# The stick-breaking mask: added in PSUM by VectorE instead of multiplied in by TensorE

## The chip, the cores and the metric

One NeuronCore of a Trainium2 chip runs one launch of the kernel. The metric is the device time in microseconds (us). Engines are named as the profile names them: TensorE (PE, its weight loads PEld), VectorE (DVE), ScalarE (ACT), GpSimd (POOL) and SyncE (SP, which here only issues DMAs).

## What is computed

A hybrid decoder layer over 512 tokens of 1024 channels, in float32. The part that the change touches is the stick-breaking branch of the attention: 8 heads of 64 channels, causal and strict (a token doesn't see itself).

```
z = q @ k.T * HEAD_DIM ** -0.5
strict = k_pos[None, :] < q_pos[:, None]
log_one_minus = where(strict, log_sigmoid(-z), 0.0)
suffix = reverse_cumsum(log_one_minus) - log_one_minus
weights = where(strict, exp(log_sigmoid(z) + suffix), 0.0)
out = weights @ v
```

Beside it stand a forgetting attention (Fox, also 8 heads, softmax with a bias of cumulative log forget gates, s <= t), the projection `x @ W_in` that makes q, k, v and the gates, the merge of both branches by gates, `W_out` and a LayerNorm, and then a feed-forward part (up projection, depthwise convolution, gelu, down projection, LayerNorm).

## The kernel before

**Products.** Every float32 operand is split in a high and a low part (`*_hi`, `*_lo`, type fp32r), and a product is three matmuls (hi hi, hi lo, lo hi; `split_product`). ScalarE writes the high parts of the weights (`high_in_order`), GpSimd the low parts (`w_lo`, L414). Weights stream in blocks of 128x1024 through four slots; SyncE loads the next block when TensorE has finished the one in its slot (`block_done`).

**Halves.** The attention runs as 8 halves, h = 0 to 7. A half is one head of each branch; two halves (e = 0, 1) make a pair of heads, and a pair's q and k rows are made while the halves before it run. Each engine has its program of a half written out by hand, and semaphores join them. In its half TensorE does, in this order: stick-breaking scores into PSUM columns 0 to 1279 (`SB_PS`), a piece of the projection (`fill(1)`), Fox scores (columns from `FX_PS`), `fill(2)`, transposes of the Fox weights (L1076), `fill(3)`, transposes of the stick-breaking weights, `fill(4)`, then the products of both branches' weights with v. The fills are the blocks of `x @ W_in` for the gates and for the next pair's q and k: 12 matmul triples in `fill(2)`. A fill's bank must have been read before it is written again (`block_read`, ScalarE: `g_all` L524 or `qk_t` L509).

**Scores.** The four query blocks r = 3, 2, 1, 0 have 512, 384, 256 and 128 keys, so a pass is four matmuls of 1280 columns in all. There are two passes: in the stick-breaking branch one with 128 rows (`sb_q`, `sb_k`: high parts stacked with low parts) and one with 64 rows (`qk_lo` with `sb_k`), in the Fox branch two with 128 rows. After each pass the mask -1e30 is added on the diagonal blocks by matmuls of `ident_bf` with `mask_bf` (`masked`, L1046): one of 256 columns after the first pass, two of 128 after the second.

**After the stick-breaking scores** (`sb_scored`) ScalarE runs Abs, Relu, Exp and Ln over 128x1280 (L544 to L549), and VectorE makes the sums (`sb_sums`, L800). VectorE's program of a half from h = 1 on is: Fox maxima (`fx_max`, L792; ScalarE needs them for the Exp into `fx_p`, L555), `sb_sums`, normalising `fx_p`, the difference L823, the split of the next pair's q and k in odd halves (`split_next`, L757 and L693), low parts of both branches' weights (L693), and at the end for b = 1 (Fox) and then b = 0 (stick-breaking) the sum of the head's output and its split (L844, L847, L693). In half 0 `sb_sums` stands ahead of `fx_max`, and ahead of both stands the split of pair 0, which ends with `fx_k` (L693).

**The stack.** When a pair's split is done (`qk_split`), SyncE copies rows from one half of the partitions to the other with four DMAs per branch (`stack`, L341 and L342: `fx_q`, `fx_k`, twice). TensorE waits for the Fox stack of a pair before the Fox scores of the pair's first half (`stack_in[1]`).

Of the kernel before, what the change touches and what calls it, by code (L numbers as in the profile page):

```python
# [21 lines left out]
P = 128  # L22
# [15 lines left out]
HALVES = 2 * PAIRS  # L38
# [76 lines left out]
def layer(nc, xT, x_tok, w_stream, w_out, cols, rows, square, out):  # L115
# [11 lines left out]
    def at(name, shape, dt, offset):  # L127
        return nc.alloc_sbuf_tensor_at(name, shape, dt, offset=offset)
# [72 lines left out]
    ident = at("ident", [P, P], f32, area_c + 2048 + 576)  # L201
    ident_bf = at("ident_bf", [P, P], bf16, area_c + 2624 + 1536)
    mask_bf = at("mask_bf", [P, 2, 2, P], bf16, area_c + 2624 + 1792)
    small = area_c + 2624 + 2816
    q_bias = at("q_bias", [P, 4 * PAIRS], f32, small)
    fx_nmax = at("fx_nmax", [P, SB], f32, small + 64)
# [16 lines left out]
    with ExitStack() as ctx:  # L223
# [5 lines left out]
        SB_PS, FX_PS = 0, 3 * 512  # L229

        def sem(name):
            return ctx.enter_context(nc.semaphore(name))
# [24 lines left out]
        v_hi_done, v_split = sem("v_hi_done"), sem("v_split")  # L257
        sel_ready = sem("sel_ready")
        sb_scored, sb_turned, sb_mixed = sem("sb_scored"), sem("sb_turned"), sem("sb_mixed")
        sb_absed, sb_relued, sb_exped, sb_lned = sem("sb_absed"), sem("sb_relued"), sem("sb_exped"), sem("sb_lned")  # L260
        sb_summed, sb_logged, sb_weighed = sem("sb_summed"), sem("sb_logged"), sem("sb_weighed")
        sb_w_hi, sb_w_split = sem("sb_w_hi"), sem("sb_w_split")
# [197 lines left out]
        def _(act):  # L460
# [75 lines left out]
            def half(h):  # L536

                pair, e = h // 2, h % 2
                scores = ps[:, SB_PS:SB_PS + FLAT]

                if h > 0:
                    act.wait_ge(sb_mixed, h)
                act.wait_ge(sb_scored, h + 1)
                nc.scalar.activation(sb_t[:], scores, ACT.Abs).then_inc(sb_absed, 1)  # L544
                nc.scalar.activation(sb_r[:], scores, ACT.Relu).then_inc(sb_relued, 1)
                act.wait_ge(sb_absed, h + 1)
                nc.scalar.activation(sb_t[:], sb_t[:], ACT.Exp, scale=-1.0).then_inc(sb_exped, 1)
                act.wait_ge(sb_exped, h + 1)
                nc.scalar.activation(sb_t[:], sb_t[:], ACT.Ln, bias=1.0).then_inc(sb_lned, 1)  # L549
                if h > 0:  # L550
                    act.wait_ge(o_split[1], h)
                act.wait_ge(fx_maxed, h * SB + SB)
                for r in range(SB):
                    off, width = QUERY_OFF[r], P * (r + 1)
                    nc.scalar.activation(fx_p[:, off:off + width], ps[:, FX_PS + off:FX_PS + off + width], ACT.Exp,  # L555
                                         bias=fx_nmax[:, r:r + 1],
                                         accum_out=fx_sum[:, r:r + 1]).then_inc(fx_exped, 1)
                fill(h, 0)
                if e == 0:

                    if h > 0:
                        act.wait_ge(fx_mixed, h)
                    for b in range(2):
                        nc.scalar.activation(v_parts[:, b, :, :, 0, :], v_of_pair(pair, b),
                                             ACT.Copy).then_inc(v_hi_done, 1)

                act.wait_ge(sb_logged, h + 1)
                nc.scalar.activation(sb_t[:], sb_t[:], ACT.Exp).then_inc(sb_weighed, 1)

                act.wait_ge(fx_turned, h + 1)  # L570
                nc.scalar.activation(fx_hi[:], ps[:, FX_PS:FX_PS + FLAT], ACT.Copy).then_inc(fx_w_hi, 1)
                fill(h, 1)
                if len(FILLS[h]) == 4 and h != TAIL:
                    fill(h, 2)
                act.wait_ge(sb_turned, h + 1)
                nc.scalar.activation(sb_hi[:], scores, ACT.Copy).then_inc(sb_w_hi, 1)
                last = 3 if len(FILLS[h]) == 4 and h != TAIL else 2
                read_fill(h, last)

                for b, mixed in ((1, fx_mixed), (0, sb_mixed)):  # L580
                    place = 512 * MIXED_BANKS[h][b]
                    act.wait_ge(mixed, h + 1)
                    if b == 0 and h > 0:
                        act.wait_ge(o_split[0], h)
                    nc.scalar.activation(o_low[b][HEAD_DIM * e:HEAD_DIM * (e + 1), :],
                                         ps[HEAD_DIM:P, place:place + 512], ACT.Copy).then_inc(o_low_done[b], 1)
                high_in_order(FIRST[h] + last + 3)
                if h == TAIL:
                    fill(h, 3)
# [101 lines left out]
        def _(dve):  # L691
# [13 lines left out]
            nc.vector.tensor_copy(ident_bf[:], sq_raw[:, 0, :])  # L705
            for side in range(2):
                nc.vector.tensor_copy(mask_bf[:, :, side, :], sq_raw[:, 1:3, :])
            nc.vector.memset(ln_eps[:], LN_EPS)
            nc.vector.memset(f_zero[:], 0.0).then_inc(const_ready, 1)
            dve.wait_ge(vb_in, 16)  # L710
# [84 lines left out]
            def sb_sums(h):  # L795
                dve.wait_ge(sb_relued, h + 1)
                dve.wait_ge(sb_lned, h + 1)
                for r in range(SB):
                    keys = slice(QUERY_OFF[r], QUERY_OFF[r] + P * (r + 1))
                    nc.vector.tensor_tensor_scan(sb_t[:, keys][:, ::-1], sb_t[:, keys][:, ::-1], sb_r[:, keys][:, ::-1],  # L800
                                                 0.0, ALU.add, ALU.add).then_inc(sb_summed, 1)

            def half(h):
                pair, e = h // 2, h % 2

                if h == 0:
                    sb_sums(h)
                    fx_max(h)
                else:
                    fx_max(h)  # L810
                    sb_sums(h)

                dve.wait_ge(fx_exped, h * SB + SB)
                if h > 0:
                    dve.wait_ge(fx_normed, h * SB)
                nc.vector.reciprocal(fx_rec[:], fx_sum[:]).then_inc(fx_inverted, 1)
                dve.wait_ge(fx_inverted, h + 1)
                for r in range(SB):
                    off, width = QUERY_OFF[r], P * (r + 1)
                    nc.vector.tensor_scalar(fx_p[:, off:off + width], fx_p[:, off:off + width],  # L820
                                            fx_rec[:, r:r + 1], None, ALU.mult).then_inc(fx_normed, 1)
                dve.wait_ge(sb_summed, (h + 1) * SB)
                nc.vector.tensor_tensor(sb_t[:], ps[:, SB_PS:SB_PS + FLAT], sb_t[:],  # L823
                                        ALU.subtract).then_inc(sb_logged, 1)

                if h < HALVES - 1:
                    select_bias(h + 1, 1 - e)
                split_next(h, 0)

                dve.wait_ge(fx_w_hi, h + 1)  # L830
                split_lo(fx_lo[:], ps[:, FX_PS:FX_PS + FLAT], fx_hi[:]).then_inc(fx_w_split, 1)
                split_next(h, 1)
                split_next(h, 2)

                dve.wait_ge(sb_w_hi, h + 1)
                split_lo(sb_lo[:], ps[:, SB_PS:SB_PS + FLAT], sb_hi[:]).then_inc(sb_w_split, 1)
                split_next(h, 3)

                rows_ = slice(HEAD_DIM * e, HEAD_DIM * (e + 1))
                for b in (1, 0):  # L840
                    place = 512 * MIXED_BANKS[h][b]
                    o_hi, o_lo = oT_hi[rows_, pair + PAIRS * b, :], oT_lo[rows_, pair + PAIRS * b, :]
                    dve.wait_ge(o_low_done[b], h + 1)
                    nc.vector.tensor_tensor(o_sum[b][rows_, :], ps[0:HEAD_DIM, place:place + 512],  # L844
                                            o_low[b][rows_, :], ALU.add).then_inc(o_added[b], 1)
                    dve.wait_ge(o_added[b], h + 1)
                    nc.vector.tensor_copy(o_hi, o_sum[b][rows_, :]).then_inc(o_hi_done[b], 1)  # L847
                    dve.wait_ge(o_hi_done[b], h + 1)
                    split_lo(o_lo, o_sum[b][rows_, :], o_hi).then_inc(o_split[b], 1)

            for h in range(HALVES):
                half(h)
# [123 lines left out]
        def _(pe):  # L976
# [72 lines left out]
            def half(h):  # L1049
# [39 lines left out]
                for q, k, first in ((sb_q[e][:], sb_k[e][:], True), (qk_lo[hd, 0, :], sb_k[e][hd, :], False)):  # L1089
                    for r in (3, 2, 1, 0):  # L1090
                        o, width = SB_PS + QUERY_OFF[r], P * (r + 1)
                        product(ps[:, o:o + width], q[:, P * r:P * (r + 1)], k[:, 0:width], start=first and r > 0)
                    last = masked(SB_PS, MASKED[0 if first else 1], 0)
                last.then_inc(sb_scored, 1)
                fill(1)

# [226 lines left out]
```

## Time and profile before

| | us |
|---|---|
| median of 3 runs | 756.11 (755.79 to 756.24) |
| the profiled execution | 756.34 |
| its span | 754.5 |
| TensorE busy | 743.8 |
| VectorE, ScalarE, GpSimd busy | 365.2, 318.3, 338.3 |

The span runs from the first to the last instruction that the profiler saw; what lies around it is 1.8 us. Half 0 begins near 78.6 us, and the last half ends near 296 us. The table's busy times are sums over the whole span. A busy TensorE is read from records with modelled ends that overlap, so two matmuls are compared by their starts.

### The profile page before, as it was taken

To read this page: it belongs to the slowest core of one execution; us is meant where nothing else is said; L and a number is where in the kernel's file an instruction comes from. 1 tells how busy PE (TensorE), PEld (TensorE's weight loads), DVE (VectorE), ACT (ScalarE), POOL (GpSimd) and SP (SyncE) were. 2 spreads that over 40 slices of the span, in tenths; PEclk is the share of its full clock that TensorE was granted. 3 is DMA by queue.
4 is the path that set the end of the run, shared out by engine and by line. 5 is a ranking of instruction groups with operands and counts; after the bars stand their busy time and mean duration, and the time that the engine had idled before them with its cause. 6 is when DMAs were issued, how large, how long until landed. Compare 5 with 4: busy or idle time off the path is not lost.

```text
span 754.5 us, 9599 instructions
## 1 busy us (share of the span) xinstructions
PE 743.8 (99%) x3528; PEld 620.7 (82%) x3528; DVE 365.2 (48%) x506; ACT 318.3 (42%) x429; POOL 338.3 (45%) x245
## 2 busy tenths in 40 slices
PE   9999999999999999999999999999999999999996
PEld 6888788888888888888899888888888888888884
DVE  3229679879879764446552112211221122322567
ACT  4323584774765775662123332323333243423410
POOL 6655254424433424992005545454544443655800
PEclk9999999999999999999999999999999999999998
DMA  8323403313214123761003322223232327332002
GB/s 300 108 84 120 132 30 112 110 56 113 85 56 135 60 75 117 279 226 56 1 1 112 101 94 92 103 87 108 84 110 83 111 83 276 115 109 86 29 29 83
DMA packets 24477, 78.33 MB, mean 104 GB/s; under 512 B 2944, under 2 KB 3328, under 8 KB 24448
## 3 DMA queue, kind: packets, MB, share of 16 engines
q1 hardware_dynamic: 24448, 77.94, 30.9%
q8 instruction: 19, 0.31, 0.2%
q14 instruction: 10, 0.08, 0.0%
HBM read 71.63 MB, written 2.10 MB: 98 GB/s over the span
## 4 chain that ended last, share of the span: by engine, by line
PE 92%; DVE 3%; ACT 1%; issue 1%; DMA 1%; POOL 0%; SPq 0%; DVEq 0%; POOLq 0%; ACTq 0%
PE ps L978 90%; PE ps L1076 2%; DVE sb_t L800 1%; PE ps L1158 0%; DMA w_raw<-w_stream_in 0%; POOL w_lo L414 0%; DVE fx_nmax L792 0%; DMA fx_k<-k_bias_rows 0%; ACT fx_p L555 0%; DVE sb_k L757 0%; DVE qk_lo L693 0%; DVE fx_lo L693 0%; DVE sb_t L823 0%; SPq L342 0%; DVE fx_k L693 0%
## 5 line engine op out<-in xcount | busy, mean ns | idle before, releaser
L414 POOL TENSOR_TENSOR w_lo<-w_raw,w_hi 128x512 fp32r<-128x512 f32 x220 | 295.6, 1366 | 374.8 <-ACT w_hi L476 368.5
L476 ACT ACTIVATE w_hi<-w_raw 128x1024 fp32r<-128x1024 f32 x109 | 115.5, 1060 | 219.0 <-DMA w_raw<-w_stream_in 218.9
L978 PE MATMUL ps<-x1T_hi,w_hi 128*128 128x512 f32 (+1 forms) x376 | 141.3, 376 | 0.0
L978 PE MATMUL ps<-x1T_hi,w_lo 128*128 128x512 f32 (+1 forms) x376 | 141.2, 376 | 0.0
L978 PE MATMUL ps<-x1T_lo,w_hi 128*128 128x512 f32 (+1 forms) x376 | 141.2, 376 | 0.0
L941 DVE SCALAR_TENSOR_TENSOR conv<-ps,col,conv 128x511 f32<-128x511 f32 (+1 forms) x44 | 33.0, 749 | 166.8 <-ACT conv L656 162.5
L978 PE MATMUL ps<-xT_hi,w_hi 128*128 128x512 f32 x264 | 105.8, 401 | 1.3 <-ACT g_all L524 1.3
L978 PE MATMUL ps<-xT_hi,w_lo 128*128 128x512 f32 x264 | 103.2, 391 | 0.0
L978 PE MATMUL ps<-xT_lo,w_hi 128*128 128x512 f32 x264 | 102.9, 390 | 0.0
L978 PEld LDWEIGHTS ps<-x1T_hi,w_hi 128*128 128x128 f32 x376 | 70.8, 188 | 12.9
L978 PEld LDWEIGHTS ps<-x1T_hi,w_lo 128*128 128x128 f32 x376 | 70.8, 188 | 12.9
L978 PEld LDWEIGHTS ps<-x1T_lo,w_hi 128*128 128x128 f32 x376 | 70.8, 188 | 12.6
L693 DVE TENSOR_TENSOR a_lo<-aT,a_hi 128x512 fp32r<-128x512 f32 x22 | 31.0, 1429 | 62.2 <-ACT a_hi L644 62.2
L978 PEld LDWEIGHTS ps<-xT_hi,w_hi 128*128 128x128 f32 x264 | 49.6, 188 | 10.9 <-ACT g_all L524 1.7
L978 PEld LDWEIGHTS ps<-xT_hi,w_lo 128*128 128x128 f32 x264 | 49.5, 188 | 10.6
L978 PEld LDWEIGHTS ps<-xT_lo,w_hi 128*128 128x128 f32 x264 | 49.7, 188 | 9.4
L978 PE MATMUL ps<-w_hi,a_lo 128*128 128x512 f32 x136 | 52.9, 389 | 0.0
L978 PE MATMUL ps<-w_hi,a_hi 128*128 128x512 f32 x136 | 52.9, 389 | 0.0
L978 PE MATMUL ps<-w_lo,a_hi 128*128 128x512 f32 x136 | 52.9, 389 | 0.0
L661 ACT ACTIVATE gelu<-conv 128x512 f32<-128x512 f32 x22 | 13.9, 632 | 41.3 <-DVE conv L941 41.3
L978 PEld LDWEIGHTS ps<-w_hi,a_lo 128*128 128x128 f32 x136 | 25.5, 188 | 5.3
L978 PEld LDWEIGHTS ps<-w_lo,a_hi 128*128 128x128 f32 x136 | 25.5, 188 | 5.3
(142 smaller groups left out, 1137.1 us busy)
## 6 DMA issues: line engine op xcount, KB each, us to landing
w_raw<-w_stream_in SPq DMA_DIRECT2D x109, 512.0 KB, 3.3
wout_raw<-w_out_in SPq DMA_DIRECT2D x8, 512.0 KB, 5.0
r_raw<-w_stream_in SPq DMA_DIRECT2D x5, 512.0 KB, 10.3
xT_raw<-xT_in SPq DMA_DIRECT2D x8, 256.0 KB, 7.1
x<-x_tok_in SPq DMA_DIRECT2D x4, 512.0 KB, 4.3
ln_rows<-rows_in SPq DMA_DIRECT2D x4, 512.0 KB, 5.5
out_dram<-x SPq DMA_DIRECT2D x8, 256.0 KB, 2.0
sb_q<-sb_q SPq DMA_DIRECT2D x8, 128.0 KB, 2.3
```

The costliest lines, as they stand in the source:

```text
L414: lo = nc.gpsimd.tensor_tensor(w_lo[:, slot, cs], w_raw[:, slot, cs], plain(w_hi[:, slot, cs]), ALU.subtract)
L476: nc.scalar.activation(w_hi[:, slot, :], w_raw[:, slot, :], ACT.Copy).then_inc(hi_ready, 1)
L661: nc.scalar.activation(gelu[:, j, :], conv[:, j, :], ACT.Gelu).then_inc(gelu_done, 1)
L693: return nc.vector.tensor_tensor(out_lo, whole, plain(part_hi), ALU.subtract)
L800: nc.vector.tensor_tensor_scan(sb_t[:, keys][:, ::-1], sb_t[:, keys][:, ::-1], sb_r[:, keys][:, ::-1], 0.0, ALU.add, ALU.add).then_inc(sb_ ...
L941: nc.vector.scalar_tensor_tensor(conv[:, j, t:SEQ], ps[:, 512 * 2 * j:512 * (2 * j + 1) - t], col[:, ds(f * CONV_WIDTH + (COL_CW + CONV_WI ...
L978: return nc.tensor.matmul(out_, lhs, rhs, start=start, stop=stop, skip_group_check=True)
L1076: last = nc.tensor.transpose(ps[:, o:o + P], weights[:, QUERY_OFF[r] + P * c:QUERY_OFF[r] + P * (c + 1)], ident[:])
```

## The change

VectorE gets a float32 copy of the mask, `sb_mask`, twice side by side. In place of the three mask matmuls of the stick-breaking scores, VectorE adds `sb_mask` to the four diagonal blocks in PSUM in two operations (`mask_sb`): blocks at columns 768 and 896, then those at 384 and 1152. ScalarE waits for both (`sb_masked`) where it waited for the scores. `mask_sb(0)` stands ahead of `sb_sums(0)`; `mask_sb(h + 1)` stands at the end of half h, between the outputs of b = 1 and b = 0. The Fox branch keeps its mask matmuls.

```diff
--- before.py
+++ after.py
@@ -201,6 +201,7 @@
     ident = at("ident", [P, P], f32, area_c + 2048 + 576)
     ident_bf = at("ident_bf", [P, P], bf16, area_c + 2624 + 1536)
     mask_bf = at("mask_bf", [P, 2, 2, P], bf16, area_c + 2624 + 1792)
+    sb_mask = at("sb_mask", [P, 2, P], f32, area_c + 2624 + 512)
     small = area_c + 2624 + 2816
     q_bias = at("q_bias", [P, 4 * PAIRS], f32, small)
     fx_nmax = at("fx_nmax", [P, SB], f32, small + 64)
@@ -257,6 +258,7 @@
         v_hi_done, v_split = sem("v_hi_done"), sem("v_split")
         sel_ready = sem("sel_ready")
         sb_scored, sb_turned, sb_mixed = sem("sb_scored"), sem("sb_turned"), sem("sb_mixed")
+        sb_masked = sem("sb_masked")
         sb_absed, sb_relued, sb_exped, sb_lned = sem("sb_absed"), sem("sb_relued"), sem("sb_exped"), sem("sb_lned")
         sb_summed, sb_logged, sb_weighed = sem("sb_summed"), sem("sb_logged"), sem("sb_weighed")
         sb_w_hi, sb_w_split = sem("sb_w_hi"), sem("sb_w_split")
@@ -540,7 +542,7 @@
 
                 if h > 0:
                     act.wait_ge(sb_mixed, h)
-                act.wait_ge(sb_scored, h + 1)
+                act.wait_ge(sb_masked, 2 * h + 2)
                 nc.scalar.activation(sb_t[:], scores, ACT.Abs).then_inc(sb_absed, 1)
                 nc.scalar.activation(sb_r[:], scores, ACT.Relu).then_inc(sb_relued, 1)
                 act.wait_ge(sb_absed, h + 1)
@@ -705,6 +707,7 @@
             nc.vector.tensor_copy(ident_bf[:], sq_raw[:, 0, :])
             for side in range(2):
                 nc.vector.tensor_copy(mask_bf[:, :, side, :], sq_raw[:, 1:3, :])
+                nc.vector.tensor_copy(sb_mask[:, side, :], sq_raw[:, 1, :])
             nc.vector.memset(ln_eps[:], LN_EPS)
             nc.vector.memset(f_zero[:], 0.0).then_inc(const_ready, 1)
             dve.wait_ge(vb_in, 16)
@@ -800,10 +803,18 @@
                     nc.vector.tensor_tensor_scan(sb_t[:, keys][:, ::-1], sb_t[:, keys][:, ::-1], sb_r[:, keys][:, ::-1],
                                                  0.0, ALU.add, ALU.add).then_inc(sb_summed, 1)
 
+            def mask_sb(h):
+
+                dve.wait_ge(sb_scored, h + 1)
+                for first, step in ((768, 128), (384, 768)):
+                    blocks = ps[:, SB_PS + first:SB_PS + first + 2 * step].rearrange("p (a c) -> p a c", a=2)[:, :, 0:P]
+                    nc.vector.tensor_tensor(blocks, blocks, sb_mask[:], ALU.add).then_inc(sb_masked, 1)
+
             def half(h):
                 pair, e = h // 2, h % 2
 
                 if h == 0:
+                    mask_sb(h)
                     sb_sums(h)
                     fx_max(h)
                 else:
@@ -847,6 +858,8 @@
                     nc.vector.tensor_copy(o_hi, o_sum[b][rows_, :]).then_inc(o_hi_done[b], 1)
                     dve.wait_ge(o_hi_done[b], h + 1)
                     split_lo(o_lo, o_sum[b][rows_, :], o_hi).then_inc(o_split[b], 1)
+                    if b == 1 and h < HALVES - 1:
+                        mask_sb(h + 1)
 
             for h in range(HALVES):
                 half(h)
@@ -1089,8 +1102,7 @@
                 for q, k, first in ((sb_q[e][:], sb_k[e][:], True), (qk_lo[hd, 0, :], sb_k[e][hd, :], False)):
                     for r in (3, 2, 1, 0):
                         o, width = SB_PS + QUERY_OFF[r], P * (r + 1)
-                        product(ps[:, o:o + width], q[:, P * r:P * (r + 1)], k[:, 0:width], start=first and r > 0)
-                    last = masked(SB_PS, MASKED[0 if first else 1], 0)
+                        last = product(ps[:, o:o + width], q[:, P * r:P * (r + 1)], k[:, 0:width], start=first and r > 0)
                 last.then_inc(sb_scored, 1)
                 fill(1)
```

TensorE at the stick-breaking scores of half 0 (`sb_k`, `sb_q` and `qk_lo` are the stacked operands, `xT` and `w` the fill behind them). Before:

```order
L978 MATMUL ps<-sb_k_81,sb_q_79 128x512
L978 MATMUL ps<-sb_k_81,sb_q_79 128x384
L978 MATMUL ps<-sb_k_81,sb_q_79 128x256
L978 MATMUL ps<-sb_k_81,sb_q_79 128x128
L978 MATMUL ps<-mask_bf,ident_bf 128x256
L978 MATMUL ps<-sb_k_81,qk_lo 128x512
L978 MATMUL ps<-sb_k_81,qk_lo 128x384
L978 MATMUL ps<-sb_k_81,qk_lo 128x256
L978 MATMUL ps<-sb_k_81,qk_lo 128x128
L978 MATMUL ps<-mask_bf,ident_bf 128x128 x2
L978 MATMUL ps<-xT_hi,w_hi 128x512
```

And in the changed kernel:

```order
L991 MATMUL ps<-sb_k_81,sb_q_79 128x512
L991 MATMUL ps<-sb_k_81,sb_q_79 128x384
L991 MATMUL ps<-sb_k_81,sb_q_79 128x256
L991 MATMUL ps<-sb_k_81,sb_q_79 128x128
L991 MATMUL ps<-sb_k_81,qk_lo 128x512
L991 MATMUL ps<-sb_k_81,qk_lo 128x384
L991 MATMUL ps<-sb_k_81,qk_lo 128x256
L991 MATMUL ps<-sb_k_81,qk_lo 128x128
L991 MATMUL ps<-xT_hi,w_hi 128x512
```

Three matmuls are gone from TensorE's queue, and nothing else has moved there; the same holds in the other seven halves.

VectorE from the split of pair 0 into half 0, and at the end of half 0. Before:

```order
L693 TENSOR_TENSOR fx_k_86<-qk_t,k_bias_rows 64x512
L800 SCALAR_TENSOR_TENSOR sb_t<-sb_t,sb_r 128x128
...
L844 TENSOR_TENSOR fx_o_sum<-ps,fx_o_low 64x512
L847 CAST oT_hi<-fx_o_sum 64x512
L693 TENSOR_TENSOR oT_lo<-fx_o_sum,oT_hi 64x512
L844 TENSOR_TENSOR sb_o_sum<-ps,sb_o_low 64x512
L847 CAST oT_hi<-sb_o_sum 64x512
L693 TENSOR_TENSOR oT_lo<-sb_o_sum,oT_hi 64x512
L792 TENSOR_REDUCE fx_nmax<-ps 128x1 x4
```

And in the changed kernel:

```order
L695 TENSOR_TENSOR fx_k_86<-qk_t,k_bias_rows 64x512
L811 TENSOR_TENSOR ps<-ps,sb_mask 128x256
L811 TENSOR_TENSOR ps<-ps,sb_mask 128x2x128
L803 SCALAR_TENSOR_TENSOR sb_t<-sb_t,sb_r 128x128
...
L855 TENSOR_TENSOR fx_o_sum<-ps,fx_o_low 64x512
L858 CAST oT_hi<-fx_o_sum 64x512
L695 TENSOR_TENSOR oT_lo<-fx_o_sum,oT_hi 64x512
L811 TENSOR_TENSOR ps<-ps,sb_mask 128x256
L811 TENSOR_TENSOR ps<-ps,sb_mask 128x2x128
L855 TENSOR_TENSOR sb_o_sum<-ps,sb_o_low 64x512
L858 CAST oT_hi<-sb_o_sum 64x512
L695 TENSOR_TENSOR oT_lo<-sb_o_sum,oT_hi 64x512
```

Two adds have come in behind `fx_k` of pair 0, and two ahead of `sb_o_sum`, for the next half's scores.

## Rows read from the trace of the kernel before

**Rows 1.** The page: the span, and TensorE's busy time with its share.
```profile
span 754.5 us, 9599 instructions
...
PE 743.8 (99%) x3528; PEld 620.7 (82%) x3528; DVE 365.2 (48%) x506; ACT 318.3 (42%) x429; POOL 338.3 (45%) x245
```

**Rows 2.** Waits of TensorE (waiter, releaser: total us, times, longest us).
```profile
PE ps L978 <- ACT g_all L524: 1.3, 1, 1.3
...
PE ps L978 <- DMA fx_k<-k_bias_rows: 0.3, 1, 0.3
```

**Rows 3.** The chain that ended last, in order of time (start us, us, what).
```profile
80.63 1.24 ACT sb_t L544
...
92.92 1.65 PE ps L978 x6
...
135.53 2.35 DMA fx_k<-k_bias_rows
```

**Rows 4.** Timeline of TensorE, half 1 (start us, us, engine, line, operation).
```profile
100.73 0.39 PE L978 MATMUL ps<-fx_hi,v_parts 128*128 128x512 f32 x1
...
101.94 0.44 PE L978 MATMUL ps<-sb_hi,v_parts 128*128 128x512 f32 x1
...
103.20 0.80 PE L978 MATMUL ps<-sb_k,sb_q 128*128 128x512 f32 x4
103.84 0.28 PE L978 MATMUL ps<-mask_bf,ident_bf 128*128 128x256 bf16 x1
104.06 0.84 PE L978 MATMUL ps<-sb_k,qk_lo 64*128 64x512 f32 x4
...
104.92 0.47 PE L978 MATMUL ps<-xT_hi,w_hi 128*128 128x512 f32 x1
...
107.75 0.74 PE L978 MATMUL ps<-k_bias_rows,q_bias_rows 128*128 128x512 f32 x4
...
109.13 0.48 PE L978 MATMUL ps<-xT_hi,w_hi 128*128 128x512 f32 x1
```

**Rows 5.** VectorE's groups by form (xcount, busy us, mean ns, idle us before).
```profile
L693 DVE TENSOR_TENSOR fx_lo<-ps,fx_hi 128x1280 fp32r<-128x1280 f32 x8 | 11.9, 1492 | 9.0 <-ACT fx_hi L571 8.9
...
L847 DVE CAST oT_hi<-sb_o_sum 64x512 fp32r<-64x512 f32 x8 | 10.5, 1315 | 0.3
...
L869 DVE TENSOR_TENSOR ps<-ps,mg_t 128x512 f32<-128x512 f32 x8 | 5.6, 700 | 0.8
...
L847 DVE CAST oT_hi<-fx_o_sum 64x512 fp32r<-64x512 f32 x8 | 3.4, 421 | 0.3
```

**Rows 6.** Timeline of VectorE: before half 0, and in half 3.
```profile
78.97 2.38 DVE L693 TENSOR_TENSOR fx_k<-qk_t,k_bias_rows 64x512 fp32r<-64x512 f32 x2
...
164.11 1.68 DVE L792 TENSOR_REDUCE fx_nmax<-ps 128x1 f32<-128x128 f32 x4 [1.07 <-PE ps L978]
165.71 2.96 DVE L800 TENSOR_TENSOR_SCAN sb_t<-sb_t,sb_r 128x128 f32<-128x128 f32 x4
```

**Rows 7.** Timeline of ScalarE at the start of half 3.
```profile
159.96 1.24 ACT L544 ACTIVATE sb_t<-ps 128x1280 f32<-128x1280 f32 x1 [0.28 <-PE ps L978]
...
163.51 1.27 ACT L549 ACTIVATE sb_t<-sb_t 128x1280 f32<-128x1280 f32 x1
```

**Rows 8.** Timeline of SyncE's DMA issues, the Fox stack of pairs 1 and 2.
```profile
133.47 1.38 SPq L342 DMA_DIRECT2D fx_k<-k_bias_rows  x1
...
189.50 0.60 SPq L342 DMA_DIRECT2D fx_k<-k_bias_rows  x1
```

**Rows 9.** Timeline of TensorE: half 4, Fox scores begin.
```profile
192.33 0.74 PE L978 MATMUL ps<-k_bias_rows,q_bias_rows 128*128 128x512 f32 x4
```

**Rows 10.** Windows: one stretch that holds most of half 0 (busy us, granted clock, DMA share, GB/s).
```profile
74.00:98.00 24.00, 22.72 (x114) 18.56 (x113) 14.49 (x26) 13.90 (x21) 7.47 (x6) 1.00 0.42 121
```

**Rows 11.** Timeline of TensorE, the kernel's first 10 us.
```profile
1.20 3.60 PE L978 MATMUL ps<-warm 128*128 128x512 bf16 x8 [1.20 <-DVE warm L696]
...
7.83 1.99 PE L978 MATMUL ps<-w_hi,xT_lo 128*128 128x512 f32 x8
```

## The prediction

> **What bounds the kernel now.** The page comes first: TensorE is busy 743.8 of 754.5 us [rows 1], so a change counts by what it does to TensorE's queue: products taken out of it, and waits put into it. The waits of TensorE come next. Inside the attention there are only two: 1.3 us once for ScalarE's `g_all`, and 0.3 us once for the DMA into `fx_k` [rows 2]. The chain of waits shows where they lie. In half 0 it leaves TensorE after the stick-breaking scores, runs through ScalarE from 80.63 us, VectorE and ScalarE again, and comes back at 92.92 us [rows 3]: everything on this path delays TensorE one for one. In half 1 it runs through VectorE's split of pair 1 to the DMA of 135.53 us, which lands 2.35 us later [rows 3]. The timelines then give the cover in the places where TensorE doesn't wait yet.
>
> **What is removed.** The trace has no score block without masks, so I take one from work of equal width. The eight products of the Fox weights with v have 2 x 1280 columns, as two score passes do; they take 101.94 - 100.73 = 1.21 us from first start to the next group's start. The Fox scores with their masks take 109.13 - 107.75 = 1.38, the stick-breaking ones 104.92 - 103.20 = 1.72 [rows 4]. So three mask products cost 0.17 us where all passes have 128 rows. In the stick-breaking block the excess is 0.51, but that holds also the change from 128 to 64 rows and back, which stays. The price of removal is between 0.17 and 0.51 per half. I take 0.24, nearer the Fox block, whose mask products are the same; a little above it, because the first mask there is followed after 104.06 - 103.84 = 0.22 us [rows 4] by a weight load that seems to have waited for it, and two waits in a row would become one. Over eight halves that is 1.9 us, if all of it reaches the end.
>
> The rule that bears on this is in the Trainium skill, page "TensorE: Matmul & The Clock Gate", section "Step-by-step: what each phase is for": a weight load's time goes by columns, and the row count doesn't matter. Taken strictly, the change of rows would be free and all of the 0.51 would belong to the masks, which is the first rival below. The trace doesn't settle it: it has no such change without a mask in between.
>
> **What is added.** Two VectorE adds of 256 columns, PSUM and SBUF into PSUM. The same form with 512 columns takes 700 ns, and a PSUM form with 1280 columns 1492 [rows 5]: 1.03 ns a column, so 0.44 us each. The second starts some 0.07 us before the record of the first ends, as other neighbours do, so the pair takes 0.8 us. The bounds are 0.6 us (2 x 256 columns at 1.03, and a little) and 1.4 us (each as long as the 512 form). The two copies into `sb_mask` in the preparation lie in front of VectorE's long wait for the first v products, and cost nothing.
>
> **Half 0: the adds stand on the path.** VectorE is in the split of pair 0 until 78.97 + 2.38 = 81.35 us [rows 6], and `mask_sb(0)` is behind it in its queue. ScalarE started Abs at 80.63. Now it starts near 81.35 + 0.8 + 0.05 = 82.2, that is 1.55 us later. All that follows waits for it in turn: ScalarE's four passes, `sb_sums`, `fx_max`, the Exp of `fx_p`, and `g_all`, whose reading frees the bank. So TensorE comes back at 94.5 instead of 92.92: **+1.55**. What half 0's own block saves only makes that wait longer: 1.3 + 1.55 + 0.24 = 3.1 us. All later work starts from the new place.
>
> **Halves 1 to 7: the adds are covered.** Take half 3. ScalarE starts Abs at 159.96 on TensorE's signal and ends Ln at 163.51 + 1.27 = 164.78 [rows 7]. Without masks the signal comes some 0.3 us sooner, VectorE stands free, and the adds take 0.8: Abs starts 0.4 to 0.5 later, Ln ends near 165.2. VectorE wants it for `sb_sums` at 165.71 - 0.24 = 165.47 [rows 6]. That is 0.27 us of cover. The stick-breaking output, which now stands behind the adds, comes 1 us later; VectorE idled 1.07 us before `fx_max` [rows 6], and part of its work there is time spent blocked beside GpSimd (the CAST of `sb_o_sum` takes 1315 ns, that of `fx_o_sum` 421 [rows 5]), which doesn't grow when it starts later. So `fx_max` still starts on TensorE's signal. Nothing is queued behind the adds that TensorE wants early: `o_added` of b = 0 is needed four triples into `fill(2)`.
>
> The second cover is the Fox stack. From `fx_max` of an odd half, VectorE works without a pause to the stack of the next pair. The last DMA of pair 2 is issued at 189.50 [rows 8] and lands 2.35 later, at 191.9; TensorE's Fox scores of half 4 start at 192.33 [rows 9]. The cover is about 0.35 after the wake-up. One saved block lies between (half 4's own), 0.24, so TensorE still doesn't wait there, nor in half 6, where the pattern repeats. In pair 1 it waited 0.3, because one issue took 1.38 us instead of 0.60 [rows 8]. I take that as an accident of the run. If it comes again, half 2's saving goes into that wait too.
>
> **Sum.** +1.55 for half 0; -0.24 x 7 = -1.7 for halves 1 to 7; -0.3 for the accidental wait. That is -0.4 against the profiled execution's 756.34, which is 0.23 above the median of the runs: 755.9. If the long issue comes again, it is +1.55 - 0.24 x 6 = +0.1, 756.4. All later stages wait for nothing on TensorE and move as a block. The product count and the VectorE count both change as meant, but the gain of TensorE is paid out in half 0.
>
> **The rivals.** *A, the masks cost all of 0.51.* For it: the excess is there, and the page's rule. Against: the Fox masks cost a third of it. Odd halves then give 0.51 each (2.04), even halves only the stack's cover of 0.35 (1.05), and the accidental wait 0.3: 1.55 - 3.4 = -1.85, 754.5. Chance 0.16.
>
> *B, GpSimd blocks the adds.* VectorE's CAST of `sb_o_sum` shows what it is to run beside `w_lo`: 0.9 us more [rows 5]. If an add with one SBUF operand does too, ScalarE starts 1 us later in half 0, and 1.1 us later in the others. There the cover of 0.27 + 0.1 is gone, and each of three Fox stacks comes 0.75 late. -0.4 + 1.0 + 2.3 = +2.9: 759.2. Against: `fx_lo`, which reads PSUM and SBUF as the adds do, has a mean of 1492 ns over all eight halves [rows 5], 1.17 ns a column, and so isn't stretched like the CAST, though GpSimd works beside some of them. It decides when the adds end over 0.3 us later than I have them. Chance 0.09.
>
> *C, the clock.* TensorE would stand still for 3.1 us in half 0, against 1.3 before, which left the granted clock at 1.00, the 2.4 GHz level [rows 10]. If it falls to 1.2 GHz, the next microseconds do half the work. The kernel's first products show the price: a group of eight takes 3.60 us at 1.20, and 1.99 at 7.83 [rows 11]; if TensorE had 5 us at half speed again, as it had between those rows, it would lose about 2.5: 758.4. No row here has so long a gap after full speed. The same page of the Trainium skill, in its section "HAM oscillation — how this bites in real kernels", warns that idle gaps between bursts bring the slow level back. Chance 0.08.
>
> *D, a mere shift:* the adds take 1.4 us, half 0 costs 2.15 and the odd halves' cover is gone by 0.3 each; +1.1, 757.3, chance 0.1 and inside the same band.
>
> **How the numbers follow.** My forecast has 0.57. A kernel's runs here differ by 0.06% and a change of 0.2% (1.5 us) is about what a measurement can tell, so "same" is 754.6 to 757.6: forecast and D. A ends at its lower edge, and I count most of A as faster; B and C are slower. That gives 0.15 faster, 0.69 same, 0.16 slower. The likeliest case's own range is 755.4 to 756.8; the range for all reaches down to A and up past D, and leaves out B and C: 754.4 to 757.9.
>
> **What would show it.** Right: TensorE's one wait for `g_all` near 3.1 us; adds of about 0.44 us at 81.3 us; stick-breaking blocks of about 1.5 us instead of 1.72; Abs in later halves 0.4 us later against the scores, and `sb_sums` not waiting; after half 0 TensorE first 1.5 us behind the kernel before, and less by 0.24 with every half. Wrong: blocks near 1.2 (A); adds over 0.8 us, or TensorE waiting for `fx_k` in three places (B); a granted clock under 1 or products at twice their spacing behind the gap (C).

## The result, and the profile after

| | before | changed |
|---|---|---|
| median | 755.44 us (22 runs, 754.86 to 757.15) | 757.97 us (22 runs, 756.31 to 760.62) |
| ratio, 95% interval | | 1.0034 (1.0027 to 1.0041) |
| profiled execution, its span | 756.34, 754.5 us | 757.42, 755.4 us |

The changed kernel is slower by 2.5 us, 0.34%. The forecast was 755.9. The first runs of the kernel before, which the forecast had, lay above its later ones: the median over 22 is 755.44. The runs of the changed kernel also spread more, over 4.3 us against 2.3.

The page of the changed kernel: the span, the busy times, the chain's shares.

```profile
span 755.4 us, 9569 instructions
...
PE 743.6 (98%) x3504; PEld 621.2 (82%) x3504; DVE 364.2 (48%) x524; ACT 318.8 (42%) x429; POOL 338.1 (45%) x245
...
PE 97%; DVE 2%; ACT 1%; issue 0%; DVEq 0%; ACTq 0%
```

TensorE has 24 matmuls fewer than in [rows 1], and its busy time has hardly fallen (743.8 to 743.6 us). The waits of TensorE:

```profile
PE ps L991 <- ACT g_all L526: 3.0, 1, 3.0
PE ps L991 <- DVE warm L698: 1.2, 1, 1.2
```

The wait for `g_all` has grown from 1.3 [rows 2] to 3.0 us, as forecast (3.1), and in this execution the wait for `fx_k` is gone. The timeline of TensorE in half 0 (start us, us, operation) shows what came behind the gap.

```profile
77.73 0.82 PE L991 MATMUL ps<-sb_k,sb_q 128*128 128x512 f32 x4
...
93.88 0.50 PE L991 MATMUL ps<-xT_hi,w_hi 128*128 128x512 f32 x1 [3.03 <-ACT g_all L526]
...
95.63 2.33 PE L1089 MATMUL ps<-ident,fx_p 128*128 128x128 f32 x10
...
100.14 1.25 PE L1089 MATMUL ps<-ident,sb_t 128*128 128x128 f32 x10
```

The same stretch in the kernel before:

```profile
78.58 0.82 PE L978 MATMUL ps<-sb_k,sb_q 128*128 128x512 f32 x4
...
92.92 0.50 PE L978 MATMUL ps<-xT_hi,w_hi 128*128 128x512 f32 x1 [1.28 <-ACT g_all L524]
...
94.41 1.25 PE L1076 MATMUL ps<-ident,fx_p 128*128 128x128 f32 x10
...
97.56 1.25 PE L1076 MATMUL ps<-ident,sb_t 128*128 128x128 f32 x10
```

From its return to the transposes of `sb_t` TensorE needed 100.14 - 93.88 = 6.26 us, where it had needed 97.56 - 92.92 = 4.64, with the same products in between: 1.62 us more. The ten transposes of `fx_p` took 2.33 us instead of 1.25; those of `sb_t` behind them took 1.25 again. The windows of TensorE (us, busy us, granted clock, DMA share, GB/s) name the cause:

```profile
85.00:90.00 5.00, 4.99 (x26) 1.00 0.24 88
90.00:92.00 2.00, 0.84 (x4) 1.00 0.01 4
92.00:94.00 2.00, 0.12 (x1) 1.00 0.72 258
94.00:96.00 2.00, 2.00 (x8) 0.76 0.00 0
96.00:98.00 2.00, 2.00 (x11) 0.50 0.00 0
98.00:100.00 2.00, 2.00 (x9) 0.88 0.00 0
100.00:102.00 2.00, 2.00 (x16) 1.00 0.00 0
```

The granted clock was 1.00 up to the gap, 0.76 on the mean of 94 to 96 us, 0.50 (the 1.2 GHz level) from 96 to 98, and was back at 1.00 at 100. A mean of 0.76 over 2 us is 0.96 us at half speed, and one of 0.88 is 0.48, so the slow stretch was 0.96 + 2.00 + 0.48 = 3.4 us long. At half speed TensorE does half the work, so it can cost up to 1.7 us. Rows 10 had 1.00 throughout, behind a gap of 1.3 us.

The adds themselves went as costed. All sixteen of them by line (ns min/median/max), and VectorE's timeline around those of half 0 and half 3:

```profile
L811 DVE TENSOR_TENSOR ps<-ps,sb_mask x16: 422/428/433, 80.6 to 269.4; 128x256 f32<-128x256 f32 x16
```

```profile
78.19 2.38 DVE L695 TENSOR_TENSOR fx_k<-qk_t,k_bias_rows 64x512 fp32r<-64x512 f32 x2
80.60 0.77 DVE L811 TENSOR_TENSOR ps<-ps,sb_mask 128x256 f32<-128x256 f32 x2
...
161.18 0.76 DVE L811 TENSOR_TENSOR ps<-ps,sb_mask 128x256 f32<-128x256 f32 x2 [0.20 <-PE ps L991]
...
165.51 1.68 DVE L795 TENSOR_REDUCE fx_nmax<-ps 128x1 f32<-128x128 f32 x4 [0.83 <-PE ps L991]
167.11 2.96 DVE L803 TENSOR_TENSOR_SCAN sb_t<-sb_t,sb_r 128x128 f32<-128x128 f32 x4
```

Each takes 0.43 us (forecast 0.44), a pair 0.77 (forecast 0.8). In half 0 they follow `fx_k` without a pause; in half 3 VectorE waits 0.20 us for the scores, makes the adds, and still idles 0.83 us before `fx_max`, so that `fx_max` starts on TensorE's signal as before. ScalarE's timeline:

```profile
81.45 1.24 ACT L546 ACTIVATE sb_t<-ps 128x1280 f32<-128x1280 f32 x1 [3.25 <-DVE ps L811]
...
162.04 1.25 ACT L546 ACTIVATE sb_t<-ps 128x1280 f32<-128x1280 f32 x1 [0.73 <-DVE ps L811]
...
165.60 1.27 ACT L551 ACTIVATE sb_t<-sb_t 128x1280 f32<-128x1280 f32 x1
```

In half 3 Ln ends at 165.60 + 1.27 = 166.87 us and the sums start at 167.11: the cover was 0.24 us, where I had 0.27. TensorE's timeline at the start of half 1:

```profile
105.79 0.80 PE L991 MATMUL ps<-sb_k,sb_q 128*128 128x512 f32 x4
106.51 0.84 PE L991 MATMUL ps<-sb_k,qk_lo 64*128 64x512 f32 x4
107.28 0.50 PE L991 MATMUL ps<-xT_hi,w_hi 128*128 128x512 f32 x1
...
110.11 0.74 PE L991 MATMUL ps<-k_bias_rows,q_bias_rows 128*128 128x512 f32 x4
```

The stick-breaking block is now 107.28 - 105.79 = 1.49 us long, against 1.72 [rows 4]: 0.23 us saved (forecast 0.24). From the first stick-breaking score to the first Fox score there were 4.55 us before [rows 4], and 4.32 now. In half 4 of this execution less was saved:

```profile
189.17 0.80 PE L991 MATMUL ps<-sb_k,sb_q 128*128 128x512 f32 x4
...
193.31 0.39 PE L991 MATMUL ps<-xT_hi,w_lo 128*128 128x512 f32 x1
193.71 0.47 PE L991 MATMUL ps<-k_bias_rows,q_bias_rows 128*128 128x512 f32 x1
```

The first Fox score starts 0.40 us behind the product in front of it, where 0.22 had been the spacing: TensorE stood 0.18 us, too short for the list of waits. The two DMAs into `fx_k` landed 2.7 and 2.8 us after their issue here, against 2.3 us at this place in the kernel before. None of the other profiles below has a wait in half 4, so this one belongs to the execution and not to the kernel.

### The profile page after: what moved, and what is told of

Read it like the earlier page. It is cut to its first block, busy times and chain, and to the rows that moved or that the text cites. A ratio compares the mean times of both kernels' runs of the same rounds, so it can differ in the third digit from the quotient of the medians.

```text
span 755.4 us, 9569 instructions
## 1 busy us (share of the span) xinstructions
PE 743.6 (98%) x3504; PEld 621.2 (82%) x3504; DVE 364.2 (48%) x524; ACT 318.8 (42%) x429; POOL 338.1 (45%) x245
## 4 chain that ended last, share of the span: by engine, by line
PE 97%; DVE 2%; ACT 1%; issue 0%; DVEq 0%; ACTq 0%
PE ps L991 94%; PE ps L1089 2%; PE ps L1170 0%; DVE sb_t L803 0%; DVE fx_k L695 0%; ACT fx_p L557 0%; DVE fx_nmax L795 0%; ACT sb_t L551 0%; ACT sb_t L546 0%; ACT sb_t L549 0%; ACT sb_r L547 0%; DVE k_bias_rows L760 0%; DVE ps L811 0%; DVE x L926 0%; DVE bn_parts L898 0%
## 5 line engine op out<-in xcount | busy, mean ns | idle before, releaser
L991 PEld LDWEIGHTS ps<-w_hi,a_hi 128*128 128x128 f32 x136 | 25.5, 188 | 5.3
```

What stands on the lines that cost most here:

```text
L991: return nc.tensor.matmul(out_, lhs, rhs, start=start, stop=stop, skip_group_check=True)
```

## The experiments

All ratios are to the kernel before, run on the same chip at the same time, with their 95% intervals. To take out how fast a run started, I also give for each profile the time from TensorE's first stick-breaking score of half 0 to its first Fox score of half 7, called the attention time; it is read off two rows of the timeline. In the same way the column "half 0" has the time from the first stick-breaking score of half 0 to that of half 1 (before: 103.20 - 78.58, changed: 105.79 - 77.73). It holds what half 0 costs, and nothing of the later halves. The experiments ran in three comparisons, in which the kernel before had medians of 755.66, 755.81 and 755.58 us, so ratios are compared and not medians.

| kernel | median us | ratio (interval) | attention us | half 0, us | half speed in half 0, us | wait for `fx_k`, pair 1 |
|---|---|---|---|---|---|---|
| before (profile ahead of the prediction) | 755.44 | | 192.37 | 24.62 | 0 | 0.3 |
| `before_again` | 756.01 | 1.0005 (0.9996 to 1.0014) | 191.86 | 24.64 | 0 | none |
| changed | 757.97 | 1.0034 (1.0027 to 1.0041) | 194.06 | 28.06 | 3.4 | none |
| `changed_again` | 758.19 | 1.0030 (1.0019 to 1.0041) | 194.98 | 28.09 | 3.4 | 0.9 |
| `half0_on_vector` | 759.51 | 1.0049 (1.0035 to 1.0064) | 196.97 | 29.31 | 6.8 | 0.2 |
| `half0_vector_filled` | 757.18 | 1.0022 (1.0014 to 1.0031) | 193.73 | 26.50 | 0 | none |
| `gap_filled` | 756.45 | 1.0012 (1.0004 to 1.0021) | 192.29 | 26.51 | 0 | none |
| `gap_part_filled` | 757.17 | 1.0019 (1.0008 to 1.0029) | 192.23 | 26.44 | 0 | none |
| `half0_on_tensor` | 754.92 | 0.9989 (0.9981 to 0.9998) | 191.29 | 24.65 | 0 | 0.7 |
| `half0_on_tensor_2` | 755.41 | 0.9996 (0.9988 to 1.0005) | 191.55 | 24.62 | 0 | 0.8 |
| `stack_first` | 754.08 | 0.9978 (0.9968 to 0.9987) | 191.70 | 24.58 | 0 | 1.1 |
| `no_masks` | 754.41 | 0.9983 (0.9974 to 0.9992) | 191.58 | 24.20 | 0 | 1.1 |
| `before_stack_first` | 755.39 | 0.9999 (0.9990 to 1.0008) | 191.77 | 24.55 | 0 | none |
| `adds_extra` | 755.40 | 0.9997 (0.9987 to 1.0007) | 191.88 | 24.63 | 0 | none |

### Was the slow stretch this kernel's, and what caused it

**changed_again**: no edit.

> The changed kernel once more, nothing edited. Theory CLOCK: the 3.0 us gap of TensorE in half 0 makes the granted clock fall to 1.2 GHz for some microseconds, and how long differs from run to run; then this profile shows a stretch at 0.50 near 95 us again, of another length or place, and the runs spread over 2 us or more around 758.0 (kernel before 755.4). Theory COVER (the rival): the adds of halves 1 to 7 and the stacks make TensorE wait in later halves; then the profile shows waits for fx_k or fx_p that the first one lacked.

It ran at 758.19, and its profile has the slow stretch again, 3.4 us long, and the wait of 3.0 us for `g_all`; but it also has a wait that the first profile lacked:

```profile
PE ps L991 <- DMA fx_k<-k_bias_rows: 0.9, 1, 0.9
```

So CLOCK held, and the rival had a part in it too. That wait is treated below. In 29 runs of the changed kernel the three with the highest mean granted clock, 0.998, were also the three shortest, 756.10, 756.31 and 756.32: some 1.7 us below the median. The mean clock of a run is a rough witness, because it also counts the idle time after the last product (in the profile of the kernel before the clock is 0.53 on the mean of 750 to 754 us). The eleven profiles without a slow stretch have means of 0.996 to 0.999, the three with one have 0.994 to 0.996. So 0.995 or less speaks for a slow stretch, 0.997 or more against it, and 0.996 says nothing. By this measure the kernel before seems to have it too, but rarely: 3 of the 93 runs in its three comparisons had 0.995, and they took 758.0 to 758.3 us.

**half0_on_tensor**: half 0 goes back to TensorE's mask products.

```diff
-                act.wait_ge(sb_masked, 2 * h + 2)
+                if h == 0:
+                    act.wait_ge(sb_scored, h + 1)
+                else:
+                    act.wait_ge(sb_masked, 2 * h)
...
                 if h == 0:
-                    mask_sb(h)
                     sb_sums(h)
...
+                    if h == 0:
+                        last = masked(SB_PS, MASKED[0 if first else 1], 0)
```

> Half 0 masked by TensorE as before, halves 1 to 7 by VectorE. CLOCK: the gap of half 0 is 1.3 us as before, the granted clock stays at 1.00, seven halves save 0.23 us each on TensorE (half 4 less): about 1.5 us under the kernel before, 753.9, runs within 1 us. COVER: no better than 757, since the adds of halves 1 to 7 are still there.

The gap was 1.3 us and the clock stayed at 1.00:

```profile
PE ps L993 <- ACT g_all L526: 1.3, 1, 1.3
...
PE ps L993 <- DMA fx_k<-k_bias_rows: 0.7, 1, 0.7
```

The kernel is no longer slower: 0.9989, and 0.9996 when repeated. That puts the whole loss in half 0. But the gain was 0.2 to 0.7 us and not the 1.5 that was expected. From score to score, odd halves are 0.22 to 0.23 us shorter than in `before_again`, halves 4 and 6 only 0.20, so that seven halves make 1.5; 0.7 to 0.8 of it went into the wait for `fx_k`. In half 4 nothing was lost here: its first Fox score follows at 0.22 us.

**half0_on_vector**: the other way round; the adds in half 0 alone, mask products in halves 1 to 7 (the conditions above turned over, and no `mask_sb` in the later halves).

> Half 0 alone masked by VectorE, halves 1 to 7 by TensorE as before. CLOCK: gap 3.0 us, the clock falls: +1.2 us for the longer way through ScalarE and +1.7 us or more for the clock, about 758.5 to 760, runs spread over 2 us. COVER: only the longer way, +1.2: 756.7.

It lost 3.7 us (1.0049). The windows, where the slow stretch is 6.8 us long (this execution took 761.19 us, 1.7 more than the median, so the stretch of a usual run may be shorter):

```profile
90.00:94.00 4.00, 1.94 (x9) 1.00 0.25 71
94.00:96.00 2.00, 1.00 (x2) 0.57 0.30 121
96.00:98.00 2.00, 2.00 (x7) 0.50 0.00 0
98.00:101.00 3.00, 3.00 (x13) 0.50 0.00 0
101.00:103.00 2.00, 2.00 (x12) 0.97 0.00 0
```

**gap_filled**: twelve products of zeros into the gap of half 0 of the changed kernel.

```diff
                 last.then_inc(fx_scored, 1)
+                if h == 0:
+                    zeros = f_zero[:].bitcast(bf16)[:, 0:512]
+                    for _ in range(12):
+                        product(bank(FILL_BANKS[0][1]), ident_bf[:], zeros)
                 fill(2)
```

> The changed kernel with twelve products of zeros (bf16, 128x512) added by TensorE to the bank of the second fill of half 0, ahead of fill 2, about 2.6 us of work that ends inside the gap. The output stays the same. CLOCK: the gap shrinks to about 0.4 us, TensorE goes on at the same moment as in the changed kernel, the clock stays at 1.00: 755.2 (the changed kernel without the slow stretch), runs within 1 us. COVER: 758, as without the filler.

The wait shrank to 0.5 us, and TensorE came back at 93.86 us, the moment at which the changed kernel came back (93.88). The windows:

```profile
92.00:94.00 2.00, 1.48 (x7) 1.00 0.00 0
94.00:96.00 2.00, 2.00 (x12) 1.00 0.81 248
96.00:98.00 2.00, 2.00 (x13) 1.00 0.04 14
98.00:100.00 2.00, 2.00 (x16) 1.00 0.00 0
```

The clock stayed at 1.00, and half 0 became 28.06 - 26.51 = 1.55 us shorter: this is the price of the slow stretch of 3.4 us, with TensorE's return at the same moment. The attention time fell by 1.77, but 0.2 of that is the wait in half 4 that the changed kernel's execution had. The ratio went from 1.0034 to 1.0012, and the runs spread over 2.4 us instead of 4.3. The median was 756.45 and not 755.2; what else half 0 cost is settled below.

**half0_vector_filled**: the same filler in half0_on_vector.

> Half 0 alone masked by VectorE, and its gap filled with twelve zero products; output unchanged. Theory CLOCK: of the 3.9 us that half0_on_vector cost over the kernel before, the longer way of half 0 is about 1.8 and the slow stretch the rest, so this one lies 1.7 to 2.2 us above the kernel before (757.4 to 757.9), granted clock 1.00 at half 0. Rival: the filler gives nothing back, 759.5.

It fell from 1.0049 to 1.0022, and half 0 became 29.31 - 26.50 = 2.81 us shorter, for a stretch twice as long. (The attention time fell by 3.24; the rest lies in the waits of pair 1.) What remains above the kernel before, 1.7 us by the ratio and 1.87 by the attention time against `before_again`, is half 0 alone: 26.50 - 24.64 = 1.86, the longer way through ScalarE.

**gap_part_filled**: four products in place of twelve, so that the gap is 2.2 us.

> The changed kernel with four zero products instead of twelve: TensorE's gap is about 2.2 us, between the 1.3 us that left the clock alone and the 3.0 us that let it fall. Output unchanged. CLOCK, in the form that the length of the gap decides: either 756.4 as with the gap filled, clock 1.00, or 758.0 with a slow stretch; I expect the first, since 2.2 us is nearer the case that was harmless, with some slow runs among them.

The profiled execution kept its clock. Of the eleven runs, four were at 758.2 to 758.7, two of them with a mean clock of 0.994 and two with 0.996, and seven at 755.7 to 757.4. This is what was expected, 2.2 us harmless in some runs and not in others, but it isn't shown: only one run was profiled, the mean clock speaks for a slow stretch in two, and the time alone doesn't decide, since a run of gap_filled took 758.04 us at 0.999.

### Do the adds of halves 1 to 7 cost anything

**adds_extra**: all mask products kept, the adds made besides in halves 1 to 7.

> All mask products stay on TensorE, and VectorE makes its adds besides in halves 1 to 7 (the mask is added twice there: -2e30 instead of -1e30, output unchanged); half 0 as in the kernel before. Theory COVERED: the adds of halves 1 to 7 cost nothing, ratio 1.000 (0.999 to 1.001), TensorE's waits as before. Rival: they make VectorE late, and waits for fx_p or fx_k appear; 757 or more.

The ratio was 0.9997, the attention time that of `before_again`, and TensorE had no wait in the attention but that of half 0 (1.3 us). From score to score each of its halves is within 0.03 us of `before_again`. The adds outside half 0 are free.

**no_masks**:

> Leaves out the stick-breaking mask altogether: no mask products on TensorE, no adds on VectorE, scores of later keys stay as they are. Theory COVERED: from half 1 on the adds cost nothing, so this lies within 0.3 us of half0_on_tensor (ratio to the kernel before 0.9989 there), about 754.8, since half 0's own saving goes into its gap. Rival NOT COVERED: the adds of halves 1 to 7 make VectorE late for the splits, and without them the kernel is 1 us or more faster still, 753.8.

0.9983 lies 0.0006 and 0.0013 under the two runs of half0_on_tensor, between the two theories. The profile separates them: in half0_on_tensor and no_masks halves 3, 4 and 5 take 29.60, 24.20, 29.61 and 29.59, 24.21, 29.62 us, with the adds and without. Taken with adds_extra, COVERED stands. What no_masks gained was in half 0, 24.20 against 24.65 us, which the expectation had at nothing; its profile lost it again in the waits for `fx_k`.

### Where the saving of TensorE went

The wait for `fx_k` of changed_again belongs to the last of these rows of SyncE's timeline of DMA issues:

```profile
136.19 0.60 SPq L344 DMA_DIRECT2D fx_k<-k_bias_rows  x1
136.83 0.60 SPq L343 DMA_DIRECT2D fx_q<-fx_q  x1
137.47 1.72 SPq L344 DMA_DIRECT2D fx_k<-k_bias_rows  x1
```

The last issue took 1.72 us instead of 0.60, as the second had taken 1.38 in [rows 8]. I had called that an accident.

**stack_first**: half0_on_tensor with the stack ahead of the weight load in SyncE's queue.

```diff
-                    load_when_free(FIRST[h] + 3 + k)
                     if h % 2 == 0 and k == 0:
                         sp.wait_ge(qk_split, pair * 4 + 4)
                         stack(1)
+                    load_when_free(FIRST[h] + 3 + k)
```

> half0_on_tensor with the four DMAs of the Fox stack issued ahead of the weight load that stood before them in SyncE's queue. Output unchanged. Theory QUEUE: the issues of 1.4 to 1.7 us and landings of 3.3 to 3.5 us in pair 1 come from the weight load in front of them; without it they take 0.6 and 2.4, TensorE's wait for fx_k (0.7 us in half0_on_tensor) is gone, and the median falls by about 0.5 us to 754.3. Rival CHANCE: the long issue is an accident of the run; nothing changes, 754.9.

The long issue was still there, with the load in front of it 6 us away, and so was the wait (1.1 us). The theory that the load in front causes it falls:

```profile
127.58 0.59 SPq L310 DMA_DIRECT2D w_raw<-w_stream_in  x1
...
133.79 1.96 SPq L344 DMA_DIRECT2D fx_k<-k_bias_rows  x1
```

The median was the best of all kernels, 754.08. To see whether the order did that:

**before_stack_first**: the same edit on the kernel before.

> The kernel before with the Fox stack issued ahead of the weight load. Output unchanged. Theory ORDER: the 0.0011 by which stack_first was ahead of half0_on_tensor comes from the order of the queue and shows here too, 755.0 against 755.8. Rival NOISE: it was the spread of the runs, and this one equals the kernel before, since the stack is released by VectorE and the load in front of it is issued long before.

0.9999: no effect there, so ORDER fails for the kernel before. For stack_first NOISE is the likelier reading, since its attention time is not below that of half0_on_tensor. It isn't shown: the interval of stack_first (up to 0.9987) just misses that of half0_on_tensor_2 (from 0.9988), and the profiled execution was 0.9 us longer than the median.

**before_again** and **half0_on_tensor_2**: no edit to either.

> The kernel before once more, nothing edited, as a control: ratio 1.000 within 0.001. Its profile shows whether the long issue of a stack DMA in pair 1 and TensorE's wait for fx_k belong to this kernel too: six of the ten profiles so far had an issue of 1.3 to 2.0 us there. Theory COMMON: a wait for fx_k between 0 and 1 us, another one than 0.3.

> half0_on_tensor again, beside its variants on one chip: ratio to the kernel before 0.9989 as before (0.998 to 1.000), clock 1.00 at half 0.

The kernel before had no long issue this time and no wait in the attention but its first:

```profile
PE ps L978 <- ACT g_all L524: 1.3, 1, 1.3
```

Over the fourteen profiles, an issue of pair 1's Fox stack took 1.3 us or more in seven. Where TensorE had its mask products in halves 1 to 7 (six profiles) that happened twice, and the wait was 0.2 to 0.3 us. Where they were gone (eight profiles) it happened five times, always at the last of the four DMAs, with waits of 0.7 to 1.1 us. So the kernel before has it too. Where it comes it costs more without the masks, which fits a TensorE that is there sooner, but in these five it was also another of the four DMAs. Whether it also makes it more frequent can't be said from 14 profiles, and what holds up the issue stays open.

## Why the prediction was wrong

**The chain, the cover, the sizes.** What bounds the kernel, where the adds stand on the path and where they are covered, was right. The adds (0.43 us each), the saved block (0.23 us), the gap (3.0 us), the cover of `sb_sums` (0.24 us) and the even start of `fx_max` came out as written.

**The step that failed** is the weighing of rival C, and with it the clock's term in the sum, which was nothing. Having worked out a gap of 3.1 us, I gave the clock 0.08, on the ground that "No row here has so long a gap after full speed", and went on with a sum in which TensorE resumes at full speed. But the clock fell to 0.50 in both profiles of the changed kernel, for 3.4 us, and in that of half0_on_vector; by gap_filled it cost 1.55 us. C's price of 2.5 us was too high, and that its time of 758.4 came near the measured 757.97 is in part luck: the other terms of the sum were 1.4 us too low, and it stands on a time 0.9 us above the median. By the Trainium skill, page "TensorE: Matmul & The Clock Gate", section "HAM oscillation — how this bites in real kernels", idle gaps between bursts bring the slow level back, and the traces agree: half speed after 3.0 us, none after 1.3.

The clock is only half of the miss. The sum was -0.45 us and +2.5 were measured; with the clock held by the filler, the changed kernel still cost 0.0012, about 0.9 us. (The forecast also stands on the profiled execution, 756.34 - 0.45 = 755.9; the 0.23 that it names was not taken off. So its distance from the median says little, and the change is what to compare.) The other terms:

**Half 0's way** measured more than +1.55. Abs started at 81.45 us, 0.88 after the end of `fx_k`, where it had started 0.72 ahead of it ([rows 3, 6]): +1.60. From Abs to TensorE's return it was 12.43 us against 12.29 [rows 3]: +0.14. From score to score the half was 26.51 us with the gap filled against 24.64, +1.87.

**Halves 1 to 7** saved 4 x 0.23 + 3 x 0.20 = 1.52 us (from score to score in gap_filled and half0_on_tensor, without the waits for `fx_k`), where I had 1.68. The blocks are 0.23 to 0.24 shorter in all of them; why the even halves give back only 0.20 is open.

**The 0.3 us wait as an accident** was wrong in kind. It comes and goes, and when it comes it takes 0.7 to 1.1 us where the masks are gone, which is what halves 1 and 2 save, and more. I had -0.3 for it. **Even halves:** I had 0.35 us of cover left at the stack and 0.24 to take from it, and that was right. At halves 4 and 6 the eight profiles without later masks have two short waits in sixteen, 0.18 and 0.23 us, both where the DMAs landed after 2.7 to 2.8 us instead of 2.35.

**The sum again,** against the median of 755.44: +1.87 for half 0, -1.52 for halves 1 to 7, +0.4 to 0.5 for the stack (five waits of about 0.9 in eight profiles, less the 0.1 that the kernel before has on the mean), +1.55 for the clock, and +0.2 that lies outside the span (757.42 - 755.4 = 2.0 us against 1.8): +2.5 to 2.6, and +2.5 measured. Without the clock it is +1.0, and gap_filled measured 0.9. The 0.2 outside the span is there in the changed kernel and its filled versions, and not in half0_on_vector; its cause stays open. The stack's term rests on few profiles.

**Rivals.** A fell: with the masks gone the block still takes 1.49 us, where eight products of the same columns and 128 rows take 1.21 (and 103.20 - 101.94 = 1.26 for the second such group) [rows 4]. The 0.23 to 0.28 belong to the change of rows, as I had argued: no kernel here has the two passes without it, but in the trace the time is lost at the two places where the rows change (last section). The rule of the Trainium skill that I had set against this (page "TensorE: Matmul & The Clock Gate", section "Step-by-step: what each phase is for") says that the time of a weight load goes by columns and not by rows, and there the trace agrees: a load took 188 to 192 ns with 128 rows and 183 to 186 with 64. My reading of it, that the change of rows would then be free, was wrong. B fell: the adds take 422 to 433 ns in all halves, although GpSimd worked beside them in each. D fell with it.

## What to carry to other kernels

When a change lengthens a stall of TensorE, ask for the clock behind it and not only for the stall: here 1.0 to 1.3 us of idling left the clock alone in all eight profiles that had them, after 2.2 us some runs look slowed, and 3.0 us slowed all three profiles, cost 1.55 us or more beyond themselves and made the runs spread. Work taken from the bounding engine is paid for where its substitute first stands on the path; here one half of eight carried all of the loss, and leaving that half as it was turned 1.0034 into 0.9989 and 0.9996. And a wait of 0.3 us on a DMA in one profile is a sample: look at it in several before it is priced.

## What the runs showed of the hardware that was not expected

- At a change from products of 128 rows to products of 64, or back, TensorE loses time. In the changed kernel's half 1 the first product behind a change started 0.15 us after a product of 128 columns, where it is 0.06 or 0.11 among products of 128 rows, and the next one came 0.33 us later, where it is 0.23 to 0.28 behind a product of 512 columns. The weight load of the first product behind a change started only with that product, while the others in this block started 0.06 us or more ahead. Without masks the two changes make the block 0.23 to 0.28 us longer (1.49 against 1.26 and 1.21).
- The slow stretch came in two lengths, 3.4 us (twice) and 6.8 us (once), and cost 1.55 and 2.81 us. In half0_on_vector the clock was already down when TensorE resumed at 95.0 us (a mean of 0.57 over 94 to 96 us is 1.7 us at half speed); in the changed kernel it fell over a microsecond after TensorE had resumed.
- A DMA issue of SyncE that takes 0.60 us took 1.3 to 2.0 us in seven of fourteen profiles, at one place of the program, without a cause that the order of the queue explains.
